# Latent attention: blocks of key and query rows turned in place and carried by GpSimd; the later layer's probabilities scaled earlier

## The chip, the cores and the metric

One core of a Trainium2 chip runs the whole program as one launch. The time is the device time of that core in microseconds; the median of 3 runs of the kernel before is 1400.31 us (1400.23 to 1400.31). The engines are TensorE (PE, matmuls and transposes into PSUM), VectorE (DVE), ScalarE (ACT), GpSimd (POOL) and SyncE (SP), which issues the weight loads. Each has its own instruction queue, worked off in order, and they meet through semaphores.

## The reference

A two layer decoder trunk on 256 tokens of width 2048, in float32. Layer A is multi-head latent attention with 16 heads, layer B a dilated sliding-window attention with 16 heads over three branches. Cut to what the change touches:

```python
# layer A: each head has 128 unrotated and 64 rotated columns
q = (rms_norm(c_q, ln_q) @ w_q_up).reshape(B, S, 16, 192)
kv = (rms_norm(c_kv, ln_kv) @ w_kv_up).reshape(B, S, 16, 256)
k = concat([kv[..., :128], broadcast(k_pe)]); v = kv[..., 128:]
q, k = rms_norm(q, g_q), rms_norm(k, g_k)
q, k = (concat([x[..., :128], rope(x[..., 128:], pos)]) for x in (q, k))
o = causal_attention(q, k, v)
h = h + (o * silu(gate)) @ w_o
# layer B: per branch g and head
s = where(valid, q_g . k_g * E**-0.5 + alibi, NEG)
p = exp(s - max(s)); den = sum(p)
o_g = (p @ v_g) / den            # then merged over g by softmax of log-denominators
h = h + (o * silu(gate)) @ w_o
```

## The kernel before

All projections are full float32 made of three passes of a reduced type: weights and activations are split in a high and a low part, and TensorE multiplies hi x hi, hi x lo and lo x hi (`three`, in `project`). The weights come in 465 steps of up to 128 x 1024 elements through a ring of four slots. For each step SyncE loads `raw` (it waits until the slot's last low part is made), ScalarE rounds `w_hi` (`highs`, L486; it waits for `slot_used`, which TensorE signals three steps earlier), VectorE subtracts for `w_lo` (`lows`, L837), and TensorE runs twelve matmuls of 512 columns. Everything else is put between these steps by hand, in the same order in each engine's program, step by step.

The latent layer goes over 8 pairs of heads (`mla_pair`, i = 0 to 7), each with 8 weight steps s: keys and values (s = 0, 1), gates (2, 3, 6, 7), queries (4, 5). The chain of a pair is, for the keys: ScalarE squares (`chain_squares` at s = 1), VectorE the mean squares (`mla_key_sums`, s = 1), GpSimd the power -0.5 (`chain`, L434), VectorE scales the rows into `rows` buffer 0 (`mla_key_rows`, s = 2) and turns their unrotated columns in 32x32 blocks in place (L1165), and ScalarE carries the sixteen blocks of 32 partitions to their places in `kT` (`mla_key_moves`, L674, spread over steps 3, 4, 7 and the next pair's 0). TensorE transposes only the rotated columns (`mla_turn` after s = 3, into `og_bank`, L1456). For the queries: squares, sums and power at s = 5, rows and rotation at s = 6 in `rows` buffer 1, and at s = 2 of the next pair TensorE transposes both the unrotated columns (four transposes into `turn`, L1453) and the rotated ones (two into `pv_bank`, L1456), which ScalarE copies to `qT` with the gain (L648) and to `q_ropes` (L651).

The attention of a pair runs in units u = 0 to 3 (head and half of the queries), from s = 3 of the next pair on: stage 0 is score (TensorE), mask and maximum (VectorE) and exponential (ScalarE), stage 1 the transpose of the probabilities (`unit_turn`, L1359) and its copy to `probT`, stage 2 the product with the values (`pv`) and the gate, stage 3 the transpose of the result. In each step the units' stages follow the projection.

The later layer has 8 pairs of 40 steps (`b_pair`, two steps to a quarter s), and `b_attend` runs the same stages at s = 2 to 7, one unit a quarter behind another. There the probabilities are scaled by the reciprocal of the denominator before they are turned: VectorE makes the reciprocal at the head of the next quarter (`b_gates`, before its `lows`), ScalarE scales in stage 1 (L738), just before `unit_turned`. For the last pair the quarters are spread over steps of the output projection (`B_LAST_SLOTS`). GpSimd has only the powers, and in the later layer a product of 128x1536 in place once a pair (`halve`, L464).

Of the kernel before, what the change touches and what calls it, by code (L numbers as in the profile page):

```python
# [114 lines left out]


KEY_MOVES = {3: range(0, 3), 4: range(3, 6), 7: range(6, 9), 8: range(9, 16)}
# [43 lines left out]
def build_program(nc, xT, x_later, x_tok, identity, consts, alibis, gains, w_in, w_pe, w_kv, w_gate_first, w_gate, w_q, w_out_a, w_b, w_out_b, out_tok):  # L161
    ctx = ExitStack()
    with ctx:
# [155 lines left out]
        key_blocks = sem("key_blocks")  # L319
        rot_step = sem("rot_step")  # L320
# [27 lines left out]
        stored = sem("stored")  # L348

# [70 lines left out]
        def _(pool):  # L420
# [20 lines left out]

            for i in range(0, PAIRS):
                for s in range(MLA_STEPS):
                    if s == 1:
                        chain(i * 2 + MLA_CHAIN_0, 2 * TILES)
                    if s == 7:
                        chain(i * 2 + (MLA_CHAIN_0 + 1), 2 * TILES)
# [25 lines left out]
        def _(act):  # L473
# [171 lines left out]
            def mla_queries_turned(par, rnd):  # L645

                act.wait_ge(turn_full, rnd + 1)
                nc.scalar.activation(qT[:, par * 512:(par + 1) * 512], turn[:], ACT.Copy, scale=gn("q_nope"))  # L648
# [15 lines left out]
            def mla_key_moves(i, par, s):  # L664

                if s == 3:
                    act.wait_ge(key_blocks, i + 1)
                for n in KEY_MOVES.get(s, ()):
                    a, b = n // 4, n % 4
                    src = rows[a * QUAD:(a + 1) * QUAD, MLA_CHAIN_0 % 2, :, 0:2 * P]\  # L670
                        .rearrange("p t (u d) -> p t u d", d=P)[:, :, :, b * QUAD:(b + 1) * QUAD]
                    dst = kT[b * QUAD:(b + 1) * QUAD, par * 768:par * 768 + 512]\
                        .rearrange("p (u t d) -> p t u d", t=TILES, d=P)[:, :, :, a * QUAD:(a + 1) * QUAD]
                    last = nc.scalar.activation(dst, src, ACT.Copy)  # L674
                    if n == 15:
                        last.then_inc(key_turned, 1)

            def mla_pair(i, par, later, steps=MLA_STEPS):
                for s in range(steps):
                    if s == 1:  # L680
                        mla_keys(i, par)
                    if s == 5:
                        chain_squares(i * 2 + (MLA_CHAIN_0 + 1), (MLA_CHAIN_0 + 1) % 2, i * MLA_STEPS + (MLA_0 + 6),
                                      KEYS_QUERIES, 384)
                    if s == 2 and later:
                        mla_queries_turned(1 - par, mla_round(i, 0))
# [6 lines left out]
                    mla_key_moves(i, par, s)  # L693
                    if s == 0 and i:
                        mla_key_moves(i - 1, 1 - par, MLA_STEPS)
# [9 lines left out]
            for k in range(OUT_STEPS):  # L705
                if k == 4:
                    mla_queries_turned(1, mla_round(PAIRS, 0))
# [11 lines left out]
                if k in (1, 2):  # L719
                    mla_key_moves(PAIRS - 1, 1, LAST_STEPS + k)  # L720
# [5 lines left out]
            def b_attend(i, s):  # L726
# [4 lines left out]
                for stage, u in b_units(s):  # L731
# [3 lines left out]
                    if stage == 1:  # L735
                        act.wait_ge(den_ready, U + 1)
                        at = prob[:, u % 2, 0:BAND]
                        nc.scalar.activation(at, at, ACT.Copy, scale=den_inv[:, u:u + 1]).then_inc(prob_scaled, 1)  # L738
                        unit_turned(b_round(i, u), u, BAND)
                    if stage == 0:  # L740
                        unit_exp(U, u, BAND)
# [90 lines left out]
        def _(dve):  # L832
# [291 lines left out]

            def mla_mask(i, u):
# [30 lines left out]
            def mla_pair(i, par, later, fill, steps=MLA_STEPS):  # L1156
                for s in range(steps):
# [4 lines left out]
                    if s == 2:  # L1162
                        dve.wait_ge(rows_ready, i * 2 + (MLA_CHAIN_0 + 1))
                        keys = rows[:, MLA_CHAIN_0 % 2, :, 0:2 * P]
# [13 lines left out]
                    elif s != 1 and (s != 4 or not par):  # L1178
                        lows((i, MLA_STEPS), MLA_0 + 4 + s, Q_STEP if s == 0 else STEP)

# [21 lines left out]
            for k in range(OUT_STEPS):  # L1202
                i, par, s = after_pairs(k)
                mla_attend(i, par, s, 2, i // 2)
                if k == 0:
                    mla_query_rows(PAIRS - 1, 1)
                    lows(OUT_A_0 + 3, OUT_A_0 + 3)
                    mla_query_rotate(PAIRS - 1)
                if k in OUT_FILL_END:
# [5 lines left out]

            def b_gates(i, s):

                for stage, u in b_units(s):
# [537 lines left out]
```

## Time and profile before

| what | before |
| --- | --- |
| median of 3 runs | 1400.31 us (1400.23 to 1400.31) |
| the profiled execution | 1400.47 us |
| its span | 1398.7 us |
| TensorE busy, matmuls | 1390.0 us (99%) |
| VectorE busy | 1038.6 us (74%) |
| ScalarE busy | 784.0 us (56%) |
| GpSimd busy | 101.5 us (7%), 67 instructions |
| latent layer | about 65 to 264 us of the span |
| later layer | about 364 to 1298 us |

Matmuls overlap in the pipeline, so TensorE's rows are to be read by the distance of their starts. In a timeline the bracket behind a row is the idle time of that engine before it, with what ended it. Durations of GpSimd are rough.

### The profile page before, as it was taken

The numbers are of one execution on the slowest core, as the hardware profiler recorded it, in microseconds if no ns is written. First come the engines' busy times: TensorE is split into PE (matmuls) and PEld (weight loads), VectorE is DVE, ScalarE is ACT, GpSimd is POOL, SyncE is SP. The second block draws the span as 40 slices with busy tenths as digits, with TensorE's granted clock in tenths as the row PEclk, the third lists the DMA queues.
The fourth block names the chain that finished last, engine by engine and source line by source line (L and its number), as shares of the span: only waits on it lengthen the run. The fifth ranks groups of instructions, "written<-read, shape, count | busy, mean of one in ns | idle before, by whom it ended". The sixth has DMA issues, their size and how long they took to land.

```text
span 1398.7 us, 17859 instructions
## 1 busy us (share of the span) xinstructions
PE 1390.0 (99%) x6584; PEld 1162.5 (83%) x6584; DVE 1038.6 (74%) x1825; ACT 784.0 (56%) x1288; POOL 101.5 (7%) x67
## 2 busy tenths in 40 slices
PE   9999999999999999999999999999999999999999
PEld 7888888888888888888888888888888888888787
DVE  6777777757677868777877886887787788688653
ACT  6577777746544654564465465446446545644642
POOL 0101001000010001000101100101010110010000
PEclk9999999999999999999999999999999999999999
DMA  9653444455556545645554654565555465456454
GB/s 356 233 174 133 162 143 140 163 187 177 183 182 211 180 156 178 209 156 180 190 185 149 199 188 157 178 209 166 161 191 192 150 196 194 151 180 198 164 167 149
DMA packets 71223, 252.40 MB, mean 180 GB/s; under 512 B 7904, under 2 KB 8288, under 8 KB 71136
## 3 DMA queue, kind: packets, MB, share of 16 engines
q1 hardware_dynamic: 70704, 249.95, 54.2%
q10 hardware_dynamic: 432, 1.31, 0.3%
q8 instruction: 52, 0.85, 0.2%
q14 instruction: 35, 0.29, 0.1%
HBM read 249.14 MB, written 2.10 MB: 180 GB/s over the span
## 4 chain that ended last, share of the span: by engine, by line
PE 94%; DVE 3%; ACT 2%; issue 1%; DMA 1%; SPq 0%; POOL 0%; DVEq 0%; ACTq 0%
PE acc L1327 86%; PE turn L1359 1%; PE score L1576 1%; DVE w_lo L837 1%; PE score L1571 1%; PE pv_bank L1591 1%; PE pv_bank L1371 1%; DVE ss L888 1%; PE score L1467 1%; PE score L1469 1%; PE pv_bank L1595 1%; DVE prob L929 1%; ACT rows L517 1%; DMA raw<-in_w_in 1%; ACT prob L738 0%
## 5 line engine op out<-in xcount | busy, mean ns | idle before, releaser
L837 DVE TENSOR_TENSOR w_lo<-raw,w_hi 128x1024 fp32r<-128x1024 f32 x463 | 573.3, 1248 | 201.9 <-ACT w_hi L486 198.0
L486 ACT ACTIVATE w_hi<-raw 128x1024 fp32r<-128x1024 f32 x463 | 482.3, 1050 | 363.4 <-PE acc L1327 355.3
L1327 PE MATMUL acc<-w_hi,xa_hi 128*128 128x512 f32 x956 | 378.5, 396 | 0.4 <-DVE w_lo L837 0.3
L1327 PE MATMUL acc<-w_hi,xa_lo 128*128 128x512 f32 x956 | 373.0, 390 | 0.0
L1327 PE MATMUL acc<-w_lo,xa_hi 128*128 128x512 f32 x956 | 372.6, 390 | 0.0
L1327 PE MATMUL acc<-w_hi,xb_hi 128*128 128x512 f32 (+1 forms) x640 | 249.5, 390 | 0.0
L1327 PE MATMUL acc<-w_hi,xb_lo 128*128 128x512 f32 (+1 forms) x640 | 245.9, 384 | 0.0
L1327 PE MATMUL acc<-w_lo,xb_hi 128*128 128x512 f32 (+1 forms) x640 | 245.6, 384 | 0.0
L1327 PEld LDWEIGHTS acc<-w_hi,xa_lo 128*128 128x128 f32 x956 | 179.4, 188 | 37.7
L1327 PEld LDWEIGHTS acc<-w_hi,xa_hi 128*128 128x128 f32 x956 | 179.7, 188 | 37.3 <-issue 0.9
L1327 PEld LDWEIGHTS acc<-w_lo,xa_hi 128*128 128x128 f32 x956 | 179.7, 188 | 35.8
L434 POOL TENSOR_TENSOR rms<-ms,mhalf 128x4 f32<-128x4 f32 (+2 forms) x50 | 73.1, 1462 | 1048.6 <-DVE ms L893 854.7
L1327 PEld LDWEIGHTS acc<-w_hi,xb_lo 128*128 128x128 f32 x640 | 120.1, 188 | 22.7
L1327 PEld LDWEIGHTS acc<-w_lo,xb_hi 128*128 128x128 f32 x640 | 120.3, 188 | 22.1
L1327 PEld LDWEIGHTS acc<-w_hi,xb_hi 128*128 128x128 f32 x640 | 120.3, 188 | 21.9
L1327 PE MATMUL acc<-w_hi,oT_hi 128*128 128x512 f32 x256 | 102.3, 400 | 0.0
L1327 PE MATMUL acc<-w_hi,oT_lo 128*128 128x512 f32 x256 | 100.0, 391 | 0.0
L1327 PE MATMUL acc<-w_lo,oT_hi 128*128 128x512 f32 x256 | 99.8, 390 | 0.0
L1238 DVE STREAM_TRANSPOSE kT<-rows 32x256 f32<-32x256 f32 (+1 forms) x256 | 94.5, 369 | 4.5
L540 ACT ACTIVATE prob<-prob,top_neg 128x128 f32<-128x128 f32 (+1 forms) x64 | 34.3, 536 | 93.0 <-DVE top_neg L934 70.9
L517 ACT ACTIVATE rows<-acc 128x512 f32<-128x512 f32 (+2 forms) x50 | 39.2, 783 | 34.3 <-PE acc L1327 34.0
L929 DVE CUSTOM_DVE_ANT_0 prob<-score,phase 64x384 f32<-64x384 f32 x64 | 35.5, 555 | 29.8 <-PE score L1576 29.4
(179 smaller groups left out, 1163.6 us busy)
## 6 DMA issues: line engine op xcount, KB each, us to landing
raw<-in_w_b SPq DMA_DIRECT2D x320, 512.0 KB, 3.8
raw<-in_w_out_a SPq DMA_DIRECT2D x32, 512.0 KB, 3.3
raw<-in_w_out_b SPq DMA_DIRECT2D x32, 512.0 KB, 3.3
raw<-in_w_gate SPq DMA_DIRECT2D x30, 512.0 KB, 3.6
raw<-in_w_kv SPq DMA_DIRECT2D x16, 512.0 KB, 4.3
raw<-in_w_in SPq DMA_DIRECT2D x15, 512.0 KB, 6.2
raw<-in_w_q SPq DMA_DIRECT2D x16, 384.0 KB, 3.0
res<-in_x_tok SPq DMA_DIRECT2D x4, 512.0 KB, 7.9
```

The costliest lines, as they stand in the source:

```text
L434: nc.gpsimd.tensor_tensor(rms[:, 0:width], ms[:, 0:width], mhalf[:, 0:width], ALU.pow)\
L486: nc.scalar.activation(w[0][:, s, 0:width], raw[:, s, 0:width], ACT.Copy).then_inc(hi_ready, 1)
L517: nc.scalar.activation(rows[:, buf, :, 0:width], acc[:, pair, :, 0:width], ACT.Square)\
L540: nc.scalar.activation(prob[:, u % 2, 0:width], prob[:, u % 2, 0:width], ACT.Exp, bias=top_neg[:, u:u + 1], accum_out=den[:, u:u + 1])\
L837: nc.vector.tensor_tensor(w[1][:, s, 0:width], raw[:, s, 0:width], w[0][:, s, 0:width].bitcast(F32), ALU.subtract).then_inc(lo_ready, 1)
L888: nc.vector.tensor_reduce(ss[:, 0, 0:n].rearrange("p (t u) -> p t u", t=TILES), rows[:, buf, :, 0:units * span].rearrange("p t (u d) -> p ...
L929: last = nc.vector.tensor_tensor_reduce(out=prob[rows_at, u % 2, 0:BAND], in0=score[rows_at, first:first + BAND], in1=bias[rows_at], scale ...
L1238: return nc.vector.transpose(dst, src)
L1327: last = nc.tensor.matmul(out, x(a), y(b), start=start and k == 0, stop=stop and k == 2, **more)
L1359: last = nc.tensor.transpose(turn[:, col:col + P], src, ident[:])
L1371: last = nc.tensor.matmul(pv, probT[:, k * P:(k + 1) * P], val, start=k == 0, stop=k == len(values) - 1)
L1467: nc.tensor.matmul(score[:, 0:n], qT[:, par * 512 + at:par * 512 + at + P], kT[:, k_0 + h * SEQ:k_0 + h * SEQ + n], start=True, stop=False)
```

## The change

For the latent layer, VectorE turns the unrotated query rows in 32x32 blocks in place too (`mla_query_blocks`, after the `lows` of s = 7), and GpSimd carries the sixteen blocks of the keys and the sixteen of the queries (`block_moves`), in its queue between the powers. ScalarE's `mla_key_moves` goes; it scales the queries by their gain in place in `qT` instead of copying them from `turn`. TensorE's `mla_turn` transposes only the rotated columns. ScalarE waits for `query_turned` before that scaling and before it writes the squares of the next queries. For the later layer, VectorE makes the reciprocal right after the mask of the same unit, waiting for the exponential, and ScalarE scales right after the exponential, waiting for the reciprocal.

```diff
@@ GpSimd
+            def block_moves(dst, rows_of, signal):
+
+                for n in range(16):
+                    a, b = n // 4, n % 4
+                    last = nc.gpsimd.tensor_copy(
+                        dst[b * QUAD:(b + 1) * QUAD].rearrange("p (u t d) -> p t u d", t=TILES, d=P)
+                        [:, :, :, a * QUAD:(a + 1) * QUAD],
+                        rows_of[a * QUAD:(a + 1) * QUAD, :, :, b * QUAD:(b + 1) * QUAD])
+                last.then_inc(signal, 1)
+
             for i in range(0, PAIRS):
-                for s in range(MLA_STEPS):
-                    if s == 1:
-                        chain(i * 2 + MLA_CHAIN_0, 2 * TILES)
-                    if s == 7:
-                        chain(i * 2 + (MLA_CHAIN_0 + 1), 2 * TILES)
+                par = i % 2
+                if i:
+                    pool.wait_ge(query_turned, i)
+                chain(i * 2 + MLA_CHAIN_0, 2 * TILES)
+                pool.wait_ge(rms_ready, i * 2 + (MLA_CHAIN_0 + 1))
+                pool.wait_ge(key_blocks, i + 1)
+                block_moves(kT[:, par * 768:par * 768 + 512], nope_rows(MLA_CHAIN_0 % 2, P), key_turned)
+                pool.wait_ge(key_turned, i + 1)
+                chain(i * 2 + (MLA_CHAIN_0 + 1), 2 * TILES)
+                pool.wait_ge(rms_ready, i * 2 + (MLA_CHAIN_0 + 2))
+                pool.wait_ge(query_blocks, i + 1)
+                block_moves(qT[:, par * 512:(par + 1) * 512], nope_rows((MLA_CHAIN_0 + 1) % 2, QK), query_turned)
+            pool.wait_ge(query_turned, PAIRS)
...
@@ ScalarE
-            def mla_queries_turned(par, rnd):
-
+            def mla_queries_turned(i, par, rnd):
+
+                act.wait_ge(query_turned, i)
+                at = qT[:, par * 512:(par + 1) * 512]
+                nc.scalar.activation(at, at, ACT.Copy, scale=gn("q_nope"))
                 act.wait_ge(turn_full, rnd + 1)
-                nc.scalar.activation(qT[:, par * 512:(par + 1) * 512], turn[:], ACT.Copy, scale=gn("q_nope"))
...
                     if s == 5:
+                        if i:
+                            act.wait_ge(query_turned, i)
                         chain_squares(i * 2 + (MLA_CHAIN_0 + 1), (MLA_CHAIN_0 + 1) % 2, i * MLA_STEPS + (MLA_0 + 6),
                                       KEYS_QUERIES, 384)
...
-                    mla_key_moves(i, par, s)
-                    if s == 0 and i:
-                        mla_key_moves(i - 1, 1 - par, MLA_STEPS)
...
                     if stage == 1:
+                        unit_turned(b_round(i, u), u, BAND)
+                    if stage == 0:
+                        unit_exp(U, u, BAND)
                         act.wait_ge(den_ready, U + 1)
                         at = prob[:, u % 2, 0:BAND]
                         nc.scalar.activation(at, at, ACT.Copy, scale=den_inv[:, u:u + 1]).then_inc(prob_scaled, 1)
-                        unit_turned(b_round(i, u), u, BAND)
-                    if stage == 0:
-                        unit_exp(U, u, BAND)
...
@@ VectorE
+            def mla_query_blocks(i):
+
+                dve.wait_ge(rows_ready, i * 2 + (MLA_CHAIN_0 + 2))
+                queries = nope_rows((MLA_CHAIN_0 + 1) % 2, QK)
+                nc.vector.transpose(queries, queries).then_inc(query_blocks, 1)
...
+                    if s == 7:
+                        mla_query_blocks(i)
...
+                if k == 1:
+                    mla_query_blocks(PAIRS - 1)
...
                     if stage == 0:
                         band_mask(U, (i - 1) * UNITS + u, u, alibi[:, u // 2, u % 2], i - 1)
+                        unit_den(U, u)
...
-                    if attend:
-                        b_gates(i, s)
...
@@ TensorE
-            def mla_turn(c, buf, rnd, rope_bank, head_step, rope_0, heads=2):
+            def mla_turn(c, buf, rnd, rope_bank, rope_0):
 
                 pe.wait_ge(rows_ready, c + 1)
                 pe.wait_ge(turn_read, rnd)
-                for h in range(heads):
-                    for t in range(TILES):
-                        nc.tensor.transpose(turn[:, h * SEQ + t * P:h * SEQ + (t + 1) * P],
-                                            rows[:, buf, t, h * head_step:h * head_step + P], ident[:])
                 for t in range(TILES):
                     last = nc.tensor.transpose(rope_bank[:, P + t * P:P + (t + 1) * P],
                                                rows[:, buf, t, rope_0:rope_0 + P], ident[:])
```

## Rows read from the trace of the kernel before

**Rows 1.** The page: span, and the chain that ended last by engine
```profile
span 1398.7 us, 17859 instructions
...
PE 94%; DVE 3%; ACT 2%; issue 1%; DMA 1%; SPq 0%; POOL 0%; DVEq 0%; ACTq 0%
```

**Rows 2.** The waits: engine, line, releaser: us in total, times, longest us
```profile
ACT w_hi L486 <- PE acc L1327: 355.3, 245, 2.5
...
PE acc L1327 <- DVE w_lo L837: 0.3, 1, 0.3
```

**Rows 3.** Timeline of TensorE in the latent layer: start us, us, instruction, count
```profile
174.03 0.60 PE L1453 MATMUL turn<-ident,rows 128*128 128x128 f32 x4
174.47 0.38 PE L1456 MATMUL pv_bank<-ident,rows 128*128 128x128 f32 x2
174.60 0.48 PE L1327 MATMUL acc<-w_hi,xa_hi 128*128 128x512 f32 x1
...
177.43 0.39 PE L1467 MATMUL score<-kT,qT 128*128 128x128 f32 x2
...
177.88 0.38 PE L1456 MATMUL og_bank<-ident,rows 128*128 128x128 f32 x2
```

**Rows 4.** Timeline of TensorE in the later layer, second unit and third
```profile
621.04 0.56 PE L1595 MATMUL pv_bank<-probT,v 128*128 128x64 f32 x4
621.82 0.55 PE L1359 MATMUL turn<-ident,prob 128*128 128x128 f32 x3 [0.22 <-ACT prob L738]
...
629.02 0.56 PE L1595 MATMUL pv_bank<-probT,v 128*128 128x64 f32 x4
629.41 0.50 PE L1359 MATMUL turn<-ident,prob 128*128 128x128 f32 x3
```

**Rows 5.** Timeline of TensorE beside the last output projection, first unit
```profile
1316.94 0.55 PE L1359 MATMUL turn<-ident,prob 128*128 128x128 f32 x3 [1.73 <-ACT prob L738]
```

**Rows 6.** Timeline of TensorE in the latent layer, second unit of a pair
```profile
156.28 0.48 PE L1371 MATMUL pv_bank<-v,probT 128*128 128x128 f32 x2
156.76 0.44 PE L1359 MATMUL turn<-ident,prob 128*128 128x128 f32 x2
```

**Rows 7.** Timelines of VectorE and ScalarE around a new pair's start
```profile
167.73 1.20 DVE L837 TENSOR_TENSOR w_lo<-raw,w_hi 128x1024 fp32r<-128x1024 f32 x1
...
169.43 0.96 DVE L837 TENSOR_TENSOR w_lo<-raw,w_hi 128x768 fp32r<-128x768 f32 x1
...
172.96 0.29 DVE L865 TENSOR_TENSOR oT_lo<-og_bank,oT_hi 128x128 fp32r<-128x128 f32 x1 [2.58 <-ACT oT_hi L550]
...
174.08 0.17 DVE L1092 TENSOR_SCALAR ms<-ss 128x4 f32<-128x4 f32 x1
175.44 0.69 DVE L907 TENSOR_TENSOR rows<-acc,rms 128x512 f32<-128x512 f32 x1 [1.19 <-POOL rms L434]
176.05 0.41 DVE L1109 TENSOR_TENSOR rows<-k_per,rms 128x256 f32<-128x256 f32 x1
...
169.42 2.22 ACT L674 ACTIVATE kT<-rows 32x128 f32<-32x128 f32 x7
```

**Rows 8.** The lines L1165 and L808: duration ns least, median, most
```profile
L1165 DVE STREAM_TRANSPOSE rows<-rows x8: 702/705/708, 75.1 to 257.6; 128x512 f32<-128x512 f32 x8
...
L808 ACT ACTIVATE kT<-kT,gain x24: 707/707/733, 471.9 to 1300.2; 128x512 f32<-128x512 f32 x24
```

**Rows 9.** Timelines of GpSimd, and of VectorE beside its product
```profile
1.27 0.53 POOL L424 MEMSET v<- 128x512 f32 x1
40.46 0.70 POOL L429 TENSOR_TENSOR r<-x_ms,mhalf 128x2 f32<-128x2 f32 x1 [38.66 <-DVE x_ms L874]
...
549.54 1.01 POOL L434 TENSOR_TENSOR rms<-ms,mhalf 128x4 f32<-128x4 f32 x1 [20.07 <-DVE ms L893]
550.52 3.70 POOL L464 TENSOR_TENSOR phase<-phase,half 128x1536 f32<-128x1536 f32 x1
...
550.39 4.91 DVE L837 TENSOR_TENSOR w_lo<-raw,w_hi 128x1024 fp32r<-128x1024 f32 x2
```

More of the change, by code:

```diff
@@ L114 @@
 QUAD = P // 4
-KEY_MOVES = {3: range(0, 3), 4: range(3, 6), 7: range(6, 9), 8: range(9, 16)}
 def b_units(s):
@@ L319, in build_program @@
         key_blocks = sem("key_blocks")
+        query_blocks = sem("query_blocks")
+        query_turned = sem("query_turned")
         rot_step = sem("rot_step")
@@ L348, in build_program, with nope_rows @@
         stored = sem("stored")
+        def nope_rows(buf, span):
+            return rows[:, buf, :, 0:2 * span].rearrange("p t (u d) -> p t u d", d=span)[:, :, :, 0:P]
         def latent_bank(c, k):
@@ L662, in mla_attend @@
                         unit_exp(pair * UNITS + u, u, mla_keys_of(u))
[L664 to L676, printed above, removed]
             def mla_pair(i, par, later, steps=MLA_STEPS):
@@ L685, in mla_pair @@
                     if s == 2 and later:
-                        mla_queries_turned(1 - par, mla_round(i, 0))
+                        mla_queries_turned(i, 1 - par, mla_round(i, 0))
                     if s == 3:
@@ L706, in _ @@
                 if k == 4:
-                    mla_queries_turned(1, mla_round(PAIRS, 0))
+                    mla_queries_turned(PAIRS, 1, mla_round(PAIRS, 0))
                 i, _, s = after_pairs(k)
@@ L718, in _ @@
                 highs(OUT_A_0 + 4 + k, OUT_A_0 + 4 + k, count=1)
-                if k in (1, 2):
-                    mla_key_moves(PAIRS - 1, 1, LAST_STEPS + k)
             def b_fill(i, par, f):
@@ L1163, in mla_pair @@
                         dve.wait_ge(rows_ready, i * 2 + (MLA_CHAIN_0 + 1))
-                        keys = rows[:, MLA_CHAIN_0 % 2, :, 0:2 * P]
+                        keys = nope_rows(MLA_CHAIN_0 % 2, P)
                         nc.vector.transpose(keys, keys).then_inc(key_blocks, 1)
@@ L1214, in _ @@
                 lows(OUT_A_0 + 4 + k, OUT_A_0 + 4 + k)
-            def b_gates(i, s):
-                for stage, u in b_units(s):
-                    if stage == 1:
-                        U = (i - 1) * UNITS + (B_UNIT_0 + u)
-                        unit_den(U, u)
             def b_blocks(f, k, n):
@@ L1306, in _ @@
             for k in range(OUT_STEPS):
-                if k + 1 in B_LAST_SLOTS:
-                    b_gates(PAIRS, B_LAST_SLOTS.index(k + 1))
                 if k in B_LAST_SLOTS:
@@ L1493, in mla_queries_turned @@
             def mla_queries_turned(i, par, rnd):
-                mla_turn((i - 1) * 2 + (MLA_CHAIN_0 + 1), (MLA_CHAIN_0 + 1) % 2, rnd, pv_bank, QK, 2 * QK)
+                mla_turn((i - 1) * 2 + (MLA_CHAIN_0 + 1), (MLA_CHAIN_0 + 1) % 2, rnd, pv_bank, 2 * QK)
             def mla_pair(i, par, later, steps=MLA_STEPS):
@@ L1516, in mla_pair @@
                     if s == 3:
-                        mla_turn(i * 2 + MLA_CHAIN_0, MLA_CHAIN_0 % 2, mla_round(i, 1) if later else 4, og_bank, P, 2 * P, 0)
+                        mla_turn(i * 2 + MLA_CHAIN_0, MLA_CHAIN_0 % 2, mla_round(i, 1) if later else 4, og_bank, 2 * P)
             latents = [tuple(x[:, c] for x in lat) for c in range(2)]
```

## The prediction

> **What bounds the kernel now.** I read the page first. TensorE is busy for the whole span and the chain that ended last is its own work [rows 1]. The view of waits comes next: ScalarE's roundings of the weights (`w_hi`, L486) wait for TensorE to free a ring slot, 355 us in all, while TensorE waited for VectorE's `w_lo` once, for 0.3 us [rows 2]. So the weight pipeline is throttled by its consumer, and an engine other than TensorE matters only where a small handshake of the attention comes late. What is left to win is (a) instructions on TensorE and (b) the few gaps in its queue, and these I looked for in its timeline, by the distance from start to start (matmuls overlap, so durations mislead: a 128x512 matmul is 0.39 long and they start every 0.23).
>
> **The change, part by part.** The profiled execution took 1400.47 us, 1.8 over its span; the median is 1400.31. I subtract from 1400.3.
>
> *Query transposes off TensorE.* Per head pair four transposes into `turn` go. They start at 174.03 and the rope transposes after them at 174.47: 0.44 us [rows 3]. There are 32 of them, eight pairs, and TensorE is saturated around each: 8 x 0.44 = 3.5 us gained.
>
> *ScalarE freed of the key moves.* Sixteen small copies a pair go, 0.32 us each (2.22 for seven) [rows 7], some 5 us of ScalarE a pair. ScalarE is not the bound, so nearly all of it is worth nothing. In three of the pairs (at 156.8, 210.5 and 264.2) three such copies stand ahead of the copy of `probT` and the exponential that TensorE wants next: there two `pv` matmuls and the transpose behind them take 0.48 us from 156.28 to 156.76 [rows 6] where, at the 0.11 us of the transposes in rows 3, they need 0.22. 3 x 0.26 = 0.8 us gained. What is added to ScalarE, the scaling of the queries in place, is SBUF to SBUF of 128x512 like the key gain of the later layer at 0.71 us [rows 8]; it takes the place of a PSUM copy of like size and stands before the wait for TensorE's rope turn, so it costs nothing if the queries are there in time (below).
>
> *Probabilities scaled early (later layer).* Before, the reciprocal sat at the head of VectorE's next step and the scaling a step later on ScalarE. In seven of the eight pairs the second unit's transpose starts 0.78 us after the last `pv` group began (621.04 to 621.82), where the third unit's needs 0.39 (629.02 to 629.41) [rows 4]; the queue in front of the scaling there holds a chain's squares, two `w_hi`, and VectorE's sum. 7 x 0.39 = 2.7 us. The last pair, beside the output projection, idles 1.73 us before its first transpose [rows 5]. After the change the scaling follows its exponential by a reciprocal and stands ahead of that queue: both gaps close, 4.4 us gained. The price: VectorE now sits through an exponential and ScalarE through a reciprocal, in 32 units. I followed one pair: `w_hi` behind the scaling comes about 0.9 us later, VectorE loses idle time that it had anyhow, the next mask starts within 0.1 us of where it did. TensorE's next weights are several us ahead. I take nought; bounds nought to 0.2 us a unit, 6 us.
>
> *VectorE's extra transpose.* One more in place block transpose of 128x512 a pair, 0.70 us [rows 8], in front of the next low parts. VectorE idles 2.58 us before the next pair's sums [rows 7], which covers it. Nought; bounds nought to 0.7 us a pair.
>
> *The copies on GpSimd.* This decides. GpSimd now has 32 copies of 32x128 a pair, 256 in all, and its queue is strict: the query copies of pair i stand ahead of the `pow` for the keys of pair i+1, the key copies ahead of the `pow` for the queries of their own pair. The second is roomy (nearly 10 us). The first is tight:
> - The `w_lo` of step 7 starts at 167.73 and ends at 168.93 [rows 7]; the new transpose ends at about 169.65, and the copies start.
> - TensorE transposes the key ropes at 177.88 [rows 3], 0.44 earlier once its transposes are gone: 177.44. Before that stand the row scaling (175.44 to 176.46, 1.02 us) and, from the end of the mean square at 174.25 to its start, 1.19 us with the `pow` in it [rows 7]. So the copies must be over by 177.44 - 1.02 - 1.19 = 175.2. The other user, the scaling and rope copies on ScalarE (0.71 + 0.76) before the score at 177.43 - 0.44, allows 175.5.
> - That is 5.6 us. One VectorE instruction with two SBUF inputs falls into it, the `w_lo` at 169.43, 0.96 us. The trace shows what such neighbours do: `w_lo` next to the 1536-element product of GpSimd, two of them, take 4.91 us [rows 9] where two take 2.4 elsewhere. They exclude each other. So 4.6 us are left for 16 copies: **0.29 us per copy** is the limit, and beyond it each of seven pairs stalls TensorE by 16 x (p - 0.29). (The first pair, without attention beside it, has about half a microsecond less.)
>
> What is p? No such copy is in the trace. From below: a memset of 512 elements takes 0.53 us, 0.13 for 128. From above: `pow` of two elements takes 0.70 and of four 1.01, which leaves 0.39 fixed at nought, and with 0.11 for the elements 0.50. The product is nearest in kind: of its 3.70 us about 1.1 are a wait for the first `w_lo` (550.52 to 551.6), 2.6 for 1536 elements read from two tensors, 1.7 ns an element; with one input half of that, 0.11 us for 128, and 0.1 to 0.15 to start and drain [rows 9]. I take 0.25: under the limit, no stall. Keeping both ends: at 0.13 nothing changes, at 0.50 the stall is 7 x 3.4 = 24 us.
>
> The Trainium skill's SBUF — State Buffer, "Who interferes with whom", calls it an exclusive lock between a GpSimd read and a VectorE instruction with two SBUF inputs; by that rule, which the 4.91 us bear out, up to one copy is also added in front of each `w_lo`. That would be 0.25 us a time on an engine that TensorE isn't waiting for, and the sum stays.
>
> **The sum.** 3.5 + 0.8 + 2.7 + 1.7 = 8.7, and 1400.3 - 8.7 = 1391.6 us.
>
> **The rivals.**
> *A. The copies are too slow.* Place: TensorE before the key ropes' turn, once a pair. The gains of 8.7 are used up at 8.7 / (7 x 16) = 0.08 above the limit, p = 0.37. Taking the product's whole 3.70 us for 1536 elements, 0.31 for 128, plus 0.1 to start, p = 0.41: stall 7 x 1.9 = 13.4, 1405.0 us. For it: a small `pow` takes 1 us, and nothing in the trace moves data from one block of partitions to another on this engine. Against it: the product's clean rate. 0.16.
> The Trainium skill's GPSIMD Engine Reference, "Elementwise — side-by-side cycle accounting", gives about 2.6 cycles an element for two inputs, an estimate of 0.28 us for 128 before any start: with 0.15 for that p would be 0.43 and the time 1407. The trace's own 1.7 ns is nearer 2 cycles, and it had two inputs.
> *B. At the edge.* p of 0.30 to 0.36: part of the stall eats part of the gain. At 0.33 it is 7 x 0.6 = 4.5, 1396.1 us. Same place, seen as a short wait before the key ropes. 0.16 for 1393.5 to 1397.5, 0.08 for within 0.2%.
> *C. The exchange in the later layer costs.* Mask, exponential, reciprocal, scaling, rounding, two low parts, in series, come by my count to 7.45 us, against TensorE's 7.5 between units. If it slips, weights come late by up to 0.2 us a unit: gains of 4.4 turn into a loss of 2, 1398. This sits inside the two last chances and takes 0.03 of each.
> **How the numbers follow.** Forecast, no or next to no stall (1390 to 1393.5): 0.60. Partly stalled but still faster by over 0.2%: 0.16. Within 0.2%, about what a measurement here can tell from no change (2.8 us): 0.08. Slower by over that: 0.16. Faster is 0.76 in all. The range runs from 1390.0, where also the first attention units' small waits go, to 1403.5, which leaves out the slow half of rival A, some 0.14, and about 0.05 below.
>
> **What the profile after would show.** Right: no transposes into `turn` from `rows`; the distance from `pv_bank` to `turn` 0.39 in all later-layer units; no 1.7 us gap at about 1310; 256 GpSimd copies starting every 0.25 us, the sixteenth of the queries over before VectorE's key mean square; TensorE's key rope turn directly behind the score. Wrong: VectorE's `rows` (L907) waits for `rms` by more than 1.2 us and TensorE idles before `og_bank` once a pair (A, B); `w_lo` of over 1.5 us in the latent layer only shows the exclusion, which is harmless; TensorE waiting for `w_lo` in the later layer is C.

## The result and the profile after

The changed kernel takes 1407.37 us (median of 4 runs, 1406.8 to 1407.7); the kernel before, run beside it, 1400.28. The ratio is 1.005 with a 95% interval of 1.0036 to 1.0063: slower by 7 us, where 1391.6 was forecast and the range ended at 1403.5. The profiled execution took 1407.43, of which the span is 1405.1, 6.4 longer than the span of [rows 1].

The page of the kernel after: span, busy time by engine, and the chain that ended last by engine.

```profile
span 1405.1 us, 17969 instructions
...
PE 1390.2 (99%) x6552; PEld 1158.2 (82%) x6552; DVE 1046.3 (74%) x1833; ACT 743.5 (53%) x1160; POOL 201.1 (14%) x323
...
PE 86%; DVE 7%; POOL 4%; issue 2%; ACT 1%; DVEq 0%; POOLq 0%
```

TensorE's share of the chain fell from 94% [rows 1] to 86%, and GpSimd, at 0% before, has 4%. "Busy 99%" says nothing of that: a wait of a microsecond between matmuls is hard to see in a share of 1405.

The view of waits of the kernel after (engine, line, releaser: us in total, times, longest us):

```profile
DVE rows L913 <- POOL rms L437: 24.9, 9, 4.8
...
ACT qT L670 <- POOL qT L449: 20.7, 8, 3.8
...
PEld turn L1365 <- ACT prob L561: 10.6, 15, 1.3
...
PE turn L1365 <- ACT prob L561: 6.9, 7, 1.0
```

VectorE waited 10.6 us in nine waits, 1.2 at most, for the same `rms` before; it now waits 24.9 in nine. And TensorE waits seven times, a microsecond each, for an exponential of the latent layer (L561), which is no line that the prediction had named.

Where the time went, from the intervals between TensorE's releases of one weight slot and the next, summed by stage (us, after less before): input projections -0.3, latent layer +11.3 (198.9 to 210.2), its output projection +0.6, later layer -3.2 (934.1 to 930.9), last output projection -2.0 (97.5 to 95.5); together 6.4, the difference of the spans. A step here is the interval that ends with its release, so what TensorE does behind step 2 counts in step 3. Within a latent pair of eight steps (steps 1, 2 and 7 changed by at most 0.05; steps 6 and 7 of pair 7 are already the first two of the output projection):

| pair | step 0 | step 3 | step 4 | step 5 | step 6 | whole pair |
|---|---|---|---|---|---|---|
| pair 0 (no attention beside it) | 0 | 0 | 0 | 0 | 0 | 20.8, as before |
| pair 1 | +0.76 | -0.41 | +1.80 | +1.21 | +0.22 | 25.3 to 28.9 |
| pairs 2, 4, 6 | 0 | -0.41 to -0.44 | +0.45 | +1.2 | +0.2 | 26.7 to 28.1 |
| pairs 3, 5, 7 | 0 | -0.41 to -0.43 | +0.45 | +1.2 | -0.1 | 26.9 to 28.1 |
| steps 5 and 6 of the output projection | | -0.41 | +1.15 | | | |

The gain (the transposes gone) stands in step 3, and right behind it in steps 4 and 5 stands a loss four times as large. What happens there shows in one pair. GpSimd's timeline of the kernel after (start us, us, instruction, count [idle before it <- releaser]):

```profile
147.38 5.94 POOL L449 COPY qT<-rows 32x128 f32<-32x128 f32 x16 [7.65 <-DVE rows L1135]
153.39 1.01 POOL L437 TENSOR_TENSOR rms<-ms,mhalf 128x4 f32<-128x4 f32 x1
...
175.45 5.97 POOL L449 COPY qT<-rows 32x128 f32<-32x128 f32 x16 [7.38 <-DVE rows L1135]
181.50 1.01 POOL L437 TENSOR_TENSOR rms<-ms,mhalf 128x4 f32<-128x4 f32 x1
```

VectorE's in the first of these pairs:

```profile
151.70 0.31 DVE L1098 TENSOR_SCALAR ms<-ss 128x4 f32<-128x4 f32 x1
154.50 0.69 DVE L913 TENSOR_TENSOR rows<-acc,rms 128x512 f32<-128x512 f32 x1 [2.50 <-POOL rms L437]
155.11 0.41 DVE L1115 TENSOR_TENSOR rows<-k_per,rms 128x256 f32<-128x256 f32 x1
155.44 0.95 DVE L843 TENSOR_TENSOR w_lo<-raw,w_hi 128x768 fp32r<-128x768 f32 x1
156.31 0.70 DVE L1177 STREAM_TRANSPOSE rows<-rows 128x512 f32<-128x512 f32 x1
156.94 1.18 DVE L843 TENSOR_TENSOR w_lo<-raw,w_hi 128x1024 fp32r<-128x1024 f32 x1
158.04 0.28 DVE L921 CUSTOM_DVE_ANT_0 prob<-score,phase 128x128 f32<-128x128 f32 x1
```

and TensorE's and ScalarE's:

```profile
154.51 0.39 PE L1333 MATMUL acc<-w_hi,xa_lo 128*128 128x512 f32 x1
154.87 0.46 PE L1469 MATMUL score<-kT,qT 128*128 128x128 f32 x2
...
159.11 0.33 PE L1365 MATMUL turn<-ident,prob 128*128 128x128 f32 x1 [0.98 <-ACT prob L561]
```

```profile
153.35 0.72 ACT L670 ACTIVATE qT<-qT,gain 128x512 f32<-128x512 f32 x1 [2.19 <-POOL qT L449]
153.98 0.75 ACT L674 ACTIVATE qT<-pv_bank 64x256 f32<-64x256 f32 x2
...
158.56 0.40 ACT L561 ACTIVATE prob<-prob,top_neg 128x128 f32<-128x128 f32 x1 [2.12 <-DVE top_neg L925]
```

The mean square of the keys is ready at 152.01 (151.70 + 0.31). GpSimd is in its copies until 153.32, so the `pow` runs from 153.39 to 154.40, and VectorE, in order, stands still for 2.5 us. Behind `rows` there stand 3.54 us of other things (154.50 to 158.04) before the mask of the next attention's first unit; then its maximum and exponential; and TensorE's transpose of that unit (L1365) comes in step 5 and waits 0.98. Scaling and rope copies on ScalarE (153.35 to 154.73) hold the score to 154.87: that is step 4's smaller loss.

The same place before the change:

```profile
147.09 0.17 DVE L1092 TENSOR_SCALAR ms<-ss 128x4 f32<-128x4 f32 x1
148.44 0.69 DVE L907 TENSOR_TENSOR rows<-acc,rms 128x512 f32<-128x512 f32 x1 [1.19 <-POOL rms L434]
...
151.99 0.28 DVE L915 CUSTOM_DVE_ANT_0 prob<-score,phase 128x128 f32<-128x128 f32 x1
...
152.50 0.40 ACT L540 ACTIVATE prob<-prob,top_neg 128x128 f32<-128x128 f32 x1 [0.82 <-DVE top_neg L919]
...
153.21 0.27 PE L1359 MATMUL turn<-ident,prob 128*128 128x128 f32 x1
```

From `rows` to the mask it is 3.55 us, as after. The exponential ends at 152.90, the transpose starts at 153.21 without a wait, 0.31 later. A transpose that does wait starts 0.15 after its exponential (after the change 158.96 to 159.11, and the same in all seven pairs). So there were 0.16 us to spare in this chain, no more (0.65 in pair 1), and the prediction never looked at it.

### The profile page after: what moved, and what is told of

It is laid out like the page before. It is cut to its first block, busy times and chain, and to the rows that moved or that the text cites. A ratio compares the mean times of both kernels' runs of the same rounds, so it can differ in the third digit from the quotient of the medians.

```text
span 1405.1 us, 17969 instructions
## 1 busy us (share of the span) xinstructions
PE 1390.2 (99%) x6552; PEld 1158.2 (82%) x6552; DVE 1046.3 (74%) x1833; ACT 743.5 (53%) x1160; POOL 201.1 (14%) x323
## 3 DMA queue, kind: packets, MB, share of 16 engines
q10 hardware_dynamic: 432, 1.31, 0.2%
## 4 chain that ended last, share of the span: by engine, by line
PE 86%; DVE 7%; POOL 4%; issue 2%; ACT 1%; DVEq 0%; POOLq 0%
PE acc L1333 79%; POOL qT L449 3%; DVE w_lo L843 3%; PE turn L1365 1%; PE pv_bank L1593 1%; PE score L1578 1%; PE score L1573 1%; PE pv_bank L1597 1%; DVE rows L913 1%; POOL rms L437 1%; POOL kT L449 1%; ACT w_hi L507 0%; PE score L1469 0%; DVE prob L921 0%; PE score L1471 0%
## 5 line engine op out<-in xcount | busy, mean ns | idle before, releaser
L561 ACT ACTIVATE prob<-prob,top_neg 128x128 f32<-128x128 f32 (+1 forms) x64 | 34.3, 536 | 117.3 <-DVE top_neg L940 73.3
L913 DVE TENSOR_TENSOR rows<-acc,rms 128x512 f32<-128x512 f32 (+2 forms) x48 | 43.5, 907 | 25.2 <-POOL rms L437 24.9
```

Source lines behind the costliest of these rows:

```text
L561: nc.scalar.activation(prob[:, u % 2, 0:width], prob[:, u % 2, 0:width], ACT.Exp, bias=top_neg[:, u:u + 1], accum_out=den[:, u:u + 1])\
L913: return nc.vector.tensor_tensor(rows[:, par, :, 0:units * span].rearrange("p t (u d) -> p t u d", u=units), acc[:, pair, :, 0:units * spa ...
```

## The experiments

All times beside the kernel before on the same chip, whose medians there were 1400.2 to 1400.4. One table first: stage times less those of the kernel before (us, from the same intervals; the input projections, -0.3 to +0.8 without a pattern, are left out), then the median and the ratio with its 95% interval.

| kernel | latent layer | its output projection | later layer | last projection | median | ratio |
|---|---|---|---|---|---|---|
| after | +11.3 | +0.6 | -3.2 | -2.0 | 1407.37 | 1.005 (1.0036 to 1.0063) |
| late_only | 0.0 | 0.0 | -3.2 | -2.0 | 1395.36 | 0.9964 (0.9951 to 0.9977) |
| half_queries | -0.6 | -0.5 | -3.2 | -2.0 | 1394.34 | 0.9955 (0.9939 to 0.9972) |
| fourteen_queries | +6.3 | 0.0 | -3.2 | -2.0 | 1401.55 | 1.0009 (1.0000 to 1.0019) |
| keys_on_act | +9.9 | +1.0 | -3.2 | -2.0 | 1405.88 | 1.0041 (1.0026 to 1.0056) |
| keys_only | +0.2 | -0.3 | -3.2 | -2.0 | 1394.93 | 0.9960 (0.9947 to 0.9974) |
| copy_price | 0.0 | 0.0 | -3.2 | -2.0 | 1395.29 | 0.9964 (0.9951 to 0.9977) |
| mask_first | +1.4 | +0.4 | -3.2 | -2.0 | 1397.24 | 0.9977 (0.9968 to 0.9987) |
| split_copies | +0.4 | -0.5 | -3.2 | -2.0 | 1395.22 | 0.9962 (0.9949 to 0.9975) |
| split_mask_first | -2.9 | -0.8 | -3.2 | -1.9 | 1391.84 | 0.9938 (0.9925 to 0.9950) |

The theory after the result: the copies of the queries end too late for the `pow` of the keys, and all of the loss is there. Rivals: copies and low parts hold each other up at the shared port; the key copies do harm as well; the exchange in the later layer costs something.

**The later layer alone (late_only).** The diff of the latent layer is undone (queries turned on TensorE, key copies on ScalarE); the part with the probabilities stays. The undone part at its core, against the changed kernel:

```diff
-                act.wait_ge(query_turned, i)
-                at = qT[:, par * 512:(par + 1) * 512]
-                nc.scalar.activation(at, at, ACT.Copy, scale=gn("q_nope"))
+                nc.scalar.activation(qT[:, par * 512:(par + 1) * 512], turn[:], ACT.Copy, scale=gn("q_nope"))
...
-                block_moves(kT[:, par * 768:par * 768 + 512], nope_rows(MLA_CHAIN_0 % 2, P), key_turned)
...
-                block_moves(qT[:, par * 512:(par + 1) * 512], nope_rows((MLA_CHAIN_0 + 1) % 2, QK), query_turned)
```

> The later layer's part alone: the latent layer is that of the kernel before, the probabilities are scaled early. The two traces put -3.2 us on the later layer and -2.0 on the last output projection. If that is this part's own gain, the time is 1395.1 us (between 1394.5 and 1395.8) and the latent layer lasts as before. If the latent part and this one act on each other, it is off that by over 1 us.

1395.36 us. The latent layer is as before to 0.01 us, each of the seven middle pairs of the later layer is 0.46 shorter (117.77 to 117.31), and one step of the last projection 1.95. Nothing in the later layer differs between this kernel and the changed one, so its whole gain and nothing of the loss comes from this part.

**Eight query copies left out (half_queries).**

```diff
-                block_moves(qT[:, par * 512:(par + 1) * 512], nope_rows((MLA_CHAIN_0 + 1) % 2, QK), query_turned)
+                block_moves(qT[:, par * 512:(par + 1) * 512], nope_rows((MLA_CHAIN_0 + 1) % 2, QK), query_turned, range(0, 16, 2))
```

> The kernel after with eight of the sixteen query copies a pair left out on GpSimd (the queries in the other blocks are stale). Theory (queue lateness): the sixteen copies end 1.5 us after the next keys' mean square, the power waits behind them, and with it the rows and the mask of the next pair's first unit, for which TensorE waits. Half the copies end before the mean square, so the stalls of 1.6 us a pair go: 1393 us (1391.5 to 1395). Rival (exclusion: copies slow VectorE's low parts): a quarter of the 256 copies goes, so a quarter of the loss: about 1404. Rival (VectorE's extra transpose is what costs): no change, 1407.

1394.34 us: 13 us less than the changed kernel for 64 copies of 0.33. In the pair at 170.8, GpSimd's timeline:

```profile
170.77 3.29 POOL L449 COPY qT<-rows 32x128 f32<-32x128 f32 x8 [7.42 <-DVE rows L1135]
175.28 1.00 POOL L437 TENSOR_TENSOR rms<-ms,mhalf 128x4 f32<-128x4 f32 x1 [1.23 <-DVE ms L1098]
```

The order is the right one again in pairs 2 to 7: GpSimd waits 1.23 us for the mean square. Step 4's loss is 0 and step 5's 0.09 to 0.13 (0.34 in pair 1, where the copies still end 0.96 after the mean square). That last tenth tells something: counted from TensorE's release of step 1, `rows` now starts 0.18 earlier than before the change (3.91 against 4.09), but TensorE arrives 0.42 earlier, and the chain had 0.16 to spare. 0.42 - 0.18 - 0.16 leaves 0.08.

Step 6 shows the same for the second unit: +0.2 in even pairs and -0.1 in odd ones, as in the changed kernel, though the copies are in time. Its transpose again starts 0.15 after its exponential ends.

**Two query copies left out (fourteen_queries).** The prediction had placed the deadline at the rope transposes and the score, a microsecond behind the mean square. By that, fourteen copies should be in time. If the deadline is the mean square itself, they are late by 0.8.

```diff
-                block_moves(qT[:, par * 512:(par + 1) * 512], nope_rows((MLA_CHAIN_0 + 1) % 2, QK), query_turned)
+                block_moves(qT[:, par * 512:(par + 1) * 512], nope_rows((MLA_CHAIN_0 + 1) % 2, QK), query_turned, range(0, 14))
```

> The kernel after with two of the sixteen query copies a pair left out (those two blocks are stale). It sits between sixteen (1407.4) and eight (1394.3). If the limit is the keys' mean square itself, that is, every moment by which the copies outlast it goes to TensorE, fourteen copies end 0.9 us after it and each of seven pairs stalls 0.9 us more than with eight: 1400.5 us (1399 to 1402). If about one more microsecond is free, as the prediction had it with its deadline at the rope turn, fourteen cost no more than eight: 1394.5 to 1396.

1401.55 us. The deadline of the prediction is refuted, by 5.5 us over the top of what it allowed. Its two users do come in time (step 4's loss is gone in pairs 2 to 7); step 5 still loses 0.91 to 0.98 in each. The timeline of VectorE shows the row scaling waiting less, but still waiting:

```profile
180.06 0.69 DVE L913 TENSOR_TENSOR rows<-acc,rms 128x512 f32<-128x512 f32 x1 [1.82 <-POOL rms L437]
```

Against the usual 1.19 of [rows 7] that is 0.63 late. Eight, fourteen and sixteen copies give 1394.3, 1401.6 and 1407.4: the last two copies, 0.66 us of work a pair, cost 5.8 us; the steps show 0.66 to 0.73 in each of eight places (pairs 1 to 7 and the output projection). So between fourteen and sixteen, beyond the deadline, every copy counts at its full price.

**The key copies back on ScalarE (keys_on_act).** Is the other half of the copies innocent?

```diff
-                pool.wait_ge(rms_ready, i * 2 + (MLA_CHAIN_0 + 1))
-                pool.wait_ge(key_blocks, i + 1)
-                block_moves(kT[:, par * 768:par * 768 + 512], nope_rows(MLA_CHAIN_0 % 2, P), key_turned)
-                pool.wait_ge(key_turned, i + 1)
...
+                    mla_key_moves(i, par, s)
+                    if s == 0 and i:
+                        mla_key_moves(i - 1, 1 - par, MLA_STEPS)
```

> The kernel after with the key copies back on ScalarE, the query copies left on GpSimd. Theory (queue lateness of the query copies): the key copies have ten microseconds and harm nothing, so the time stays at 1407.4, plus nought to 3 where ScalarE's copies come before the squares again. Rival (the number of GpSimd copies, through exclusion or through lateness of the queries' power): half of the copies goes, the time falls below 1403.

1405.88 us, 1.5 less than the changed kernel, where the theory allowed 1407.4 or more. The steps 4 and 5 of pairs 2 to 7 are the same to 0.06. The rival that saw the harm in the key copies falls, but the key copies aren't free either: step 0 of pair 1 is 0.76 shorter without them and step 4 there 1.0. In pair 0 no attention runs beside, the whole pair takes 20.8 us and not 26.8, and the `pow` for the queries really stands behind the sixteen key copies. GpSimd in the changed kernel, first pair and second:

```profile
75.68 8.05 POOL L449 COPY kT<-rows 32x128 f32<-32x128 f32 x16 [2.76 <-DVE rows L1177]
83.81 1.01 POOL L437 TENSOR_TENSOR rms<-ms,mhalf 128x4 f32<-128x4 f32 x1
91.30 5.80 POOL L449 COPY qT<-rows 32x128 f32<-32x128 f32 x16 [6.48 <-DVE rows L1135]
97.19 1.01 POOL L437 TENSOR_TENSOR rms<-ms,mhalf 128x4 f32<-128x4 f32 x1
```

The `pow` follows the copies with no idle time, and VectorE's wait for the one at 97.19 is the longest of all, 4.8 us.

**The queries back on TensorE (keys_only).** The complement: GpSimd carries the keys, TensorE transposes the queries.

```diff
-                block_moves(qT[:, par * 512:(par + 1) * 512], nope_rows((MLA_CHAIN_0 + 1) % 2, QK), query_turned)
...
+                for h in range(heads):
+                    for t in range(TILES):
+                        nc.tensor.transpose(turn[:, h * SEQ + t * P:h * SEQ + (t + 1) * P],
+                                            rows[:, buf, t, h * head_step:h * head_step + P], ident[:])
```

> The kernel after with the queries undone: TensorE transposes their unrotated columns again, GpSimd carries the keys alone. Theory (query lateness): all stalls behind the query copies go, the 3.5 us of TensorE's transposes come back, and the 0.8 us that the first pair loses to its key copies stays: 1395.7 us (1394.8 to 1396.6), that is late_only within a microsecond. Rival (GpSimd's copies beside VectorE cost by their number): half of the latent loss stays, 1401.

1394.93 us, 0.4 under late_only, the intervals overlapping. The steps tell more than the median: pair 1 loses 0.73 in step 0, and pairs 3, 5 and 7 gain 0.3 each in step 6, the one where three key copies had stood on ScalarE ahead of `probT` and the exponential (pair 7's step 6 is the first of the output projection). Steps 4 and 5 are untouched. The moves of the keys are a wash of -0.9 and +0.7; the loss of the changed kernel needs the queries.

**The price of a copy, by itself (copy_price).** Base late_only; in the third pair of the later layer, where GpSimd is idle, 64 more copies on a scratch tensor: four groups of 16, over to another block of partitions (32x128), within the same block (32x128), then 32x64 and 32x32.

```diff
+            def price(kind, shift, width, parts=QUAD):
+                for turn in range(4):
+                    pool.wait_ge(priced, kind * 4 + turn + 1)
+                    for q in range(P // parts):
+                        there, here = q * parts, (q * parts + shift) % P
+                        last = nc.gpsimd.tensor_copy(
+                            scratch[there:there + parts, 128:128 + width].rearrange("p (u d) -> p u d", u=4),
+                            scratch[here:here + parts, 0:width].rearrange("p (u d) -> p u d", u=4))
+                    last.then_inc(priced, 1)
```

> The later layer's part alone, and 64 GpSimd copies more in the later layer's third pair, on scratch memory, in groups of four: 32 partitions to another block x128, to the same block x128, to another x64, to another x32. If a copy of 32x128 is 0.33 us by a fixed start, the x64 comes at 0.27 or more and the x32 at 0.24 or more, and same block is as another. If it is by the elements (2.6 ns each), x64 comes at 0.17 and x32 at 0.09. If crossing blocks costs, the same block is faster, under 0.25. The time: as late_only within 0.3 us if exclusion is harmless beside a slack of microseconds; over 1 us more if it isn't.

1395.29 us, against late_only's 1395.36: 24 us of GpSimd's copies (the busy times below) beside VectorE's low parts cost nothing. The groups of GpSimd (busy us, mean ns of one | idle before):

```profile
L475 POOL COPY scratch<-scratch 32x128 f32<-32x128 f32 x32 | 14.8, 464 | 1.5
L475 POOL COPY scratch<-scratch 32x64 f32<-32x64 f32 x16 | 5.5, 343 | 0.7
L475 POOL COPY scratch<-scratch 32x32 f32<-32x32 f32 x16 | 3.3, 203 | 0.7
```

These means mix undisturbed copies with some that stood behind a low part. Undisturbed, from start to start, a copy takes 0.326 us at 128 elements, to another block or not, 0.27 at 64 and 0.24 at 32: 0.9 ns an element ((0.326 - 0.242) / 96) and 0.21 us whatever the size. In the changed kernel itself the median from start to start is 0.330 over 240 intervals. VectorE next to them, in the same stretch:

```profile
593.67 2.54 DVE L859 TENSOR_TENSOR w_lo<-raw,w_hi 128x1024 fp32r<-128x1024 f32 x2
...
599.96 2.51 DVE L859 TENSOR_TENSOR w_lo<-raw,w_hi 128x1024 fp32r<-128x1024 f32 x2
```

2.54 and 2.51 for two low parts where two take 2.4 to 2.5 elsewhere. By itself a low part takes at most 1.31 instead of 1.23 us, while a copy caught beside one takes 1.1 to 1.3 us. This run shows it only in the later layer, where VectorE has microseconds of slack. For the latent layer keys_only (128 copies) and mask_first (all 256) say it: step 5 loses nothing there. The port as the cause of the loss falls.

**The mask of unit 0 ahead (mask_first).** If the loss goes through the exponential, it must vanish when the exponential no longer stands behind the whole of the keys' work, though the copies stay late. VectorE's order is changed for that: the keys' block transpose and step 2's low part go behind the mask. All work is done.

```diff
-                    if s == 2:
+                    if s == 3:
                         dve.wait_ge(rows_ready, i * 2 + (MLA_CHAIN_0 + 1))
...
-                    elif s != 1 and (s != 4 or not par):
+                    elif s == 3:
+                        lows((i, MLA_STEPS), MLA_0 + 6)
+                        lows((i, MLA_STEPS), MLA_0 + 7)
+                    elif s not in (1, 2) and (s != 4 or not par):
```

> The kernel after with one change of order on VectorE: the keys' block transpose and the low part of step s = 2 come behind the mask of the next unit 0 in s = 3, not ahead of it. All copies stay. Theory: of the 1.6 us a pair, 1.2 is the first unit's transpose waiting for an exponential whose mask stands behind these two instructions; that part goes, and 0.4 (score and rope turn) stays: 1400 us (1398.5 to 1401.5). If the exponential is late for another reason, or exclusion is the cost, the time stays at 1407.

1397.24 us, 10 less than the changed kernel and 1.3 better than the range given. VectorE and, below the dots, TensorE:

```profile
151.78 0.69 DVE L913 TENSOR_TENSOR rows<-acc,rms 128x512 f32<-128x512 f32 x1 [2.49 <-POOL rms L437]
...
153.58 0.28 DVE L921 CUSTOM_DVE_ANT_0 prob<-score,phase 128x128 f32<-128x128 f32 x1
```

```profile
155.24 0.27 PE L1368 MATMUL turn<-ident,prob 128*128 128x128 f32 x1
```

VectorE waits 2.49 us for `rms` as in the changed kernel, the mask comes 1.8 us after `rows` and not 3.5, and TensorE's transpose has no idle time before it. Step 5's loss is 0.00 in every pair. Step 4's stays (0.38 to 0.46 in pairs 2 to 7, 1.80 in pair 1, 1.14 in the output projection), which shows that this part goes another way: over the scaling on ScalarE to the score. What I had not counted is step 6: it is 0.2 shorter than in the changed kernel in every pair from 1 on (the second unit's exponential is now in time too), so that pairs 3, 5 and 7 show the 0.3 from ScalarE's freed queue.

**Ten copies on GpSimd, six on ScalarE (split_copies).** The other cure: leave VectorE's order, and bring the copies under the deadline.

```diff
-                block_moves(qT[:, par * 512:(par + 1) * 512], nope_rows((MLA_CHAIN_0 + 1) % 2, QK), query_turned)
+                block_moves(qT[:, par * 512:(par + 1) * 512], nope_rows((MLA_CHAIN_0 + 1) % 2, QK), query_turned, range(0, 10))
...
+            def mla_query_moves(i, par):
+
+                act.wait_ge(query_blocks, i + 1)
+                for n in range(10, 16):
...
+                    if s == 0 and i:
+                        mla_query_moves(i - 1, 1 - par)
```

> The kernel after with the last six of the sixteen query copies of a pair on ScalarE, in its idle two microseconds of step s = 0; GpSimd makes ten. Nothing is left out. Theory: ten copies at 0.33 us and one w_lo are 4.3 us, just over before the mean square at 4.5, so the stall goes as with half_queries: 1394.3 us (1393 to 1395.5). If ScalarE's copies push its squares back, each 0.3 us of it costs 2 us in all.

1395.22 us. GpSimd in one pair:

```profile
144.33 3.96 POOL L450 COPY qT<-rows 32x128 f32<-32x128 f32 x10 [7.63 <-DVE rows L1153]
148.88 1.01 POOL L438 TENSOR_TENSOR rms<-ms,mhalf 128x4 f32<-128x4 f32 x1 [0.59 <-DVE ms L1116]
```

The `pow` waits for the mean square again (0.59), step 4's loss is 0, step 5's 0.11 to 0.20, but 1.03 in pair 1. There ScalarE's six copies (91.64 to 93.54) stand right before the squares of the keys (93.56), and the mean square ends 3.22 us after TensorE's release of step 1, not 1.87 as in the changed kernel. That is the risk that the expectation named.

**Both (split_mask_first).** The two diffs above together; all work is done.

> split_copies and the order of mask_first together, all work done. Theory: TensorE keeps 3.5 us for its 32 transposes, the first unit's wait of 0.1 us a pair goes too, and the first pair's 0.8 us stays: 1392.6 us (1391.6 to 1394), under late_only by 1.4 or more. If the limit after the copies is elsewhere, it is late_only's 1395.4 again.

1391.84 us (1391.6 to 1392.0), ratio 0.9938: faster than the kernel before (1400.40 beside it) by 8.6 us, and than each part alone. Steps 4 and 5 lose nothing in any pair, step 3 gains 0.40 to 0.42 in each, step 6 0.3 in every second, and 0.77 is left in step 0 of pair 1. That is near the 1391.6 that the prediction had for the change, but not by the same terms: the later layer gives 5.2 and not 4.4, and step 0 of pair 1 takes 0.8 back. Nor do copies in time suffice: half_queries and split_copies, without the new order on VectorE, end at 1394.3 and 1395.2.

## Why the prediction was wrong

*The price of a copy.* I took 0.25 and kept 0.13 to 0.50; it is 0.33. The part by element was right (0.11 us for 128, measured 0.9 ns an element), the start too small: 0.10 to 0.15, measured 0.21. `pow` had bounded it at 0.39. The Trainium skill's GPSIMD Engine Reference, "Elementwise — side-by-side cycle accounting", gives 1.03 cycles an element for the leanest loop, by estimate 0.86 ns at the 1.2 GHz of its example, beside the 2.6 for two inputs that I had quoted. The measured 0.9 ns agrees with the former; the figure for two inputs was the wrong one to hold against a copy.

*The deadline.* This is the step that failed: "the copies must be over by 177.44 - 1.02 - 1.19 = 175.2", and from it the limit of 0.29 us a copy. With 0.33 the prediction's own formula, 7 x 16 x (0.33 - 0.29), gives its rival B, 1396.1 us, not 1407.4: the size of p explains 4.5 us, and 11 are left. The limit of 0.29 had come from the two users of the copies' result and of the key rope: the rope transposes and the score. Measured at those users, the loss in pairs 2 to 7 is 0.45 a pair, near the 0.6 of the formula. But the `pow` serves the whole of VectorE's queue behind `rows`, and I followed only the instructions that use the keys, not those that merely stand behind them. One of these, the mask of unit 0, leads to a transpose that had 0.16 us to spare, and TensorE now came 0.42 earlier. So the real deadline is the keys' mean square itself. From the start of the copies (175.45) to that (179.93) are 4.5 us, of which the low parts take 0.7 (16 copies in 5.97 where 16 x 0.33 = 5.3); 3.8 / 16 = 0.24 is the limit. Even the 0.25 of the forecast would have been just over it.

*What it sums to.* Step 5 loses 1.2 in seven pairs, 8.4. One pair's 1.2 + 0.45 = 1.65 can be worked out: counted from TensorE's release of step 1, `rows` starts 5.41 to 5.47 us behind it in pairs 2 to 7, where it was 4.09 before the change, so it is late by 1.35; TensorE arrives 0.42 earlier; 0.16 were to spare. 1.35 + 0.42 - 0.16 = 1.61. The same three terms give 0.90 for fourteen copies (measured 0.91 to 0.98), 0.08 for eight (0.09 to 0.13), and in pair 1 of the changed kernel, with 0.65 to spare, 3.1 (3.0). The mean square itself is not later than before: 2.65 to 2.92 us after that release, against 2.90. Step 4 loses 2.7 in pairs 2 to 7, 1.8 in pair 1 and 1.15 in the output projection; step 0 of pair 1 0.8. Together 14.9 lost. Gained: 3.4 in step 3 and 5.2 in the later layer. Step 6 is +0.4 on balance, the input projections -0.3. 14.9 - 8.6 + 0.4 - 0.3 = 6.4, as the spans differ.

*Query transposes off TensorE, 3.5.* Right: 0.40 to 0.45 in each of eight places, 3.4.

*ScalarE freed of the key moves, 0.8.* Right in size and place, as keys_only and split_mask_first show (0.3 in each of the three places, 0.9). In the changed kernel only 0.1 of each is left, and the even pairs lose 0.2: the second unit's transpose waits for its exponential there. Since half_queries and split_copies show the same, this is not the lateness of the copies but TensorE's earlier arrival meeting VectorE's order, which keys_only and mask_first each take away. The prediction had no such term.

*Probabilities scaled early, 2.7 + 1.7.* Right in mechanism, a little small in size. 7 x 0.46 = 3.2 and 2.0 were measured. TensorE in the changed kernel, a second unit of the later layer and the unit of [rows 5]:

```profile
632.18 0.56 PE L1597 MATMUL pv_bank<-probT,v 128*128 128x64 f32 x4
632.57 0.50 PE L1365 MATMUL turn<-ident,prob 128*128 128x128 f32 x3
...
1323.46 0.49 PE L1365 MATMUL turn<-ident,prob 128*128 128x128 f32 x3
```

0.39 from one to the next, where [rows 4] had 0.78, and no idle time where [rows 5] had 1.73. The exchange between VectorE and ScalarE (rival C) cost nothing that TensorE saw.

*VectorE's extra transpose, nought.* Nothing contradicts it: 0.70 us beside idle time, and split_mask_first, which has it, has no loss left in steps 3 to 7. It wasn't tried by itself.

*"The second is roomy (nearly 10 us)".* True of pairs 1 to 7, wrong of pair 0, where the steps are shorter: the `pow` of its queries stood behind its key copies, 0.76 us for TensorE in step 0 of pair 1, and part of the 1.80 in step 4.

*The rivals.* A had the sign and, with 1405.0, almost the time, but by luck: its price of 0.41 isn't there; B had the price and the place of a good third of the loss (step 4, 5.7 of 14.9). The right case, B's price with an earlier deadline, was in neither. Of the signs named for the profile after, two spoke for A or B (waits of `rows` over 1.2 us, copies not over before the mean square); the idle time of TensorE was not before `og_bank` but before `score` and, mainly, `turn` from `prob`.

## What to carry to other kernels

Work put in front of a small step of an in-order engine is due when the *input* of that step is ready, unless every instruction behind its result, on every engine queue that waits for it, has slack: follow the queue, not only the data. Look for the least slack at the next thing TensorE waits for (here 0.16 us, in a unit that has nothing to do with the copies), and take off it what the same change makes TensorE arrive earlier (0.42, which alone was more than the slack). If a helper engine is late, try both cures: give it less ahead of the handshake, and move what the handshake holds up out of the way of the next one. Here either alone was 3.4 us or more short of both (1395.2 and 1397.2 against 1391.8).

## What the runs showed of the hardware

- A GpSimd copy of 32x128 fp32 costs 0.33 us from start to start; 0.21 of it does not depend on size. To another block of 32 partitions it costs the same as within one. Sixteen small pieces therefore pay 3.4 us of 5.3 for the part that does not depend on size.
- The exclusion between a GpSimd instruction and a low part is lopsided. A copy that meets a low part takes 1.0 to 1.4 us in the changed kernel (1.1 to 1.3 in copy_price), where one by itself takes 0.29; a low part that meets a row of copies takes at most 0.12 longer (1.34 against 1.23 us in the changed kernel, 1.31 in copy_price). Beside one long product two low parts took 4.91 us instead of 2.4 [rows 9], which is the product's whole 2.6 more. The Trainium skill's SBUF — State Buffer, "Who interferes with whom", calls this an exclusive lock, held by whoever issues first for its whole instruction, and the numbers fit.
- VectorE's own small instructions feel it too: beside the copies the addition to the sum of squares and the mean square took, at most, 0.28 and 0.31 us where they take 0.17 each. Why isn't settled here. From the start of the first to the end of the second that was 0.26 us more in the pair at 151 us and 0.10 in the pair at 179.
